# Attention of a two-block model on one core: values stationary, turned weights as the moving operand, one of three head groups in the other row half

## The reference, cut to what matters

```python
# first block, per layer: 3 groups of 8 heads of 64, group g dilated by 1, 4, 16
logits = einsum(q, k) * 64 ** -0.5 + bias; masked outside the window and off the stride
m = max(logits); p = exp(logits - m); s = sum(p); o = (p @ v) / s; lse = m + log(s)
alpha = softmax over the 3 groups of lse;  o = sum_g alpha_g * o_g     # 8 heads x 64
# second block: 16 query heads of 64 on 4 key/value heads, a window of 3 chunks of 64,
sc = q @ k.T * 64 ** -0.5 + bias;  p = softmax([sc, sink])[..., :-1];  o = p @ v
```

## Time and profile before

| | |
|---|---|
| median of 3 runs | 2090.59 us (2090.15 to 2091.51) |
| profiled execution, span | 2088.1 us (no other time is given of it) |
| TensorE busy | 99% |
| VectorE / ScalarE busy | 69% / 49% |
| block 1's attention | about 342 to 461 us and 1059 to 1173 us |
| block 2's attention | about 1682 to 1792 us |

### The profile page before, as it was taken

One profiled execution on the slowest core, in us unless ns is written; L12 is line 12 of the kernel. 1 busy time (PEld: TensorE's weight loads), 2 busy tenths in 40 slices (PEclk: granted clock), 3 DMA queues, 4 the chain that ended last, 5 costly groups with the idle time before them and its releaser, 6 DMA issues.

```text
span 2088.1 us, 28981 instructions
## 1 busy us (share of the span) xinstructions
PE 2057.4 (99%) x11649; PEld 1788.4 (86%) x11649; DVE 1432.8 (69%) x1822; ACT 1028.6 (49%) x1279; POOL 36.5 (2%) x78
## 2 busy tenths in 40 slices
PE   7999999999999999999999999999999999999998
PEld 7788888999888888888899998888788799998887
DVE  5887787668777677767866786455654568756454
ACT  4443544444544363445444445444644668646443
POOL 0000000000000000000000000000000010000000
PEclk9999999999999999999999999999999999999999
DMA  9887688447688758868865485654755454456652
GB/s 320 269 286 249 194 287 249 128 145 252 222 263 264 247 164 280 263 202 260 288 185 144 144 300 194 199 188 144 228 195 182 137 161 137 162 184 210 195 188 81
DMA packets 355929, 438.04 MB, mean 210 GB/s; under 512 B 9571, under 2 KB 323371, under 8 KB 355796
## 3 DMA queue, kind: packets, MB, share of 16 engines
q1 hardware_dynamic: 350592, 420.51, 61.8%
q0 software_dynamic: 4160, 14.23, 3.1%
q10 hardware_dynamic: 1044, 1.46, 0.2%
HBM read 435.05 MB, written 1.11 MB: 209 GB/s over the span
## 4 chain that ended last, share of the span: by engine, by line
PE 86%; DVE 6%; ACT 4%; DMA 2%; issue 1%; DVEq 1%; SPq 0%; ACTq 0%
PE PC L1808 7%; PE PC L1810 7%; PE PC L1809 6%; PE PA L1808 6%; PE PA L1810 6%; PE PA L1809 6%; PE PB L1808 6%; PE PB L1810 6%; PE PB L1809 6%; PE PA L1801 4%; PE PA L1802 4%; PE PA L1803 4%; PE PC L1839 3%; DVE lo L1172 2%; PE PC L1801 2%; PE PC L1976 2%
## 5 line engine op out<-in xcount | busy, mean ns | idle before, releaser
L1172 DVE TENSOR_TENSOR lo<-raw,hi 128x2048 fp32r<-128x2048 f32 x274 | 626.7, 2289 | 209.3 <-ACT hi L696 208.4
L696 ACT ACTIVATE hi<-raw 128x2048 fp32r<-128x2048 f32 x277 | 529.2, 1911 | 260.5 <-PE PC L1810 115.2
L1198 DVE SCALAR_TENSOR_TENSOR acc<-raw,cs,acc 128x256 f32<-128x256 f32 x448 | 217.1, 485 | 34.4 <-issue 0.9
L1808 PE MATMUL PA<-hi,nn 128*128 128x512 f32 (+1 forms) x528 | 210.0, 398 | 6.7 <-DVE nn L1274 5.6
L1801 PE MATMUL PA<-nn,hi 128*128 128x256 f32 x720 | 209.0, 290 | 0.4 <-ACT f L1089 0.4
L1810 PE MATMUL PA<-hi,nn 128*128 128x512 f32 (+1 forms) x528 | 205.6, 389 | 0.0
L1809 PE MATMUL PA<-lo,nn 128*128 128x512 f32 (+1 forms) x528 | 205.1, 388 | 0.0
L1802 PE MATMUL PA<-nn,lo 128*128 128x256 f32 x720 | 203.6, 283 | 0.0
L1803 PE MATMUL PA<-nn,hi 128*128 128x256 f32 x720 | 203.5, 283 | 0.0
L1808 PE MATMUL PB<-hi,nn 128*128 128x512 f32 x400 | 157.5, 394 | 0.6 <-DVE nn L1274 0.6
L1810 PE MATMUL PB<-hi,nn 128*128 128x512 f32 x400 | 156.0, 390 | 0.0
(11 more groups left out here) (317 smaller groups left out, 4086.8 us busy)
## 6 DMA issues: line engine op xcount, KB each, us to landing
raw<-in_w_in SPq DMA_DIRECT2D x90, 1024.0 KB, 5.3
raw<-in_ada_w SPq DMA_DIRECT2D x66, 1024.0 KB, 7.2
raw<-in_ffn_w_gate SPq DMA_DIRECT2D x88, 512.0 KB, 4.1
raw<-in_ffn_w_up SPq DMA_DIRECT2D x88, 512.0 KB, 5.2
raw<-in_ffn_w_down SPq DMA_DIRECT2D x44, 1024.0 KB, 5.3
raw<-in_ffn_w SPq DMA_DIRECT2D x88, 512.0 KB, 4.8
raw<-in_ffn_w SPq DMA_DIRECT2D x22, 1024.0 KB, 4.9
raw<-in_w_o SPq DMA_DIRECT2D x12, 1024.0 KB, 6.4
```

Source lines behind the costliest of these rows:

```text
L696: A(parts_of(n)[0], raw[:, n % 3, :], ACT.Copy).then_inc(hi_done, 1)
L1172: V.tensor_tensor(l, raw[:, n % 3, :], h.bitcast(F32), ALU.subtract).then_inc(lo_done, 1)
L1198: i = V.scalar_tensor_tensor(o, w[:, k, :], cs[:, k:k + 1], o, ALU.mult, ALU.add)
L1808: MM(o, xl, wh[:, c0:c0 + w], start=first, stop=False, skip_group_check=True)
```

## The change

The logits of group 1 (the middle one) are computed in the other row half of the array: the 256-column units of w_in that make its q and k have each pair of 64-column blocks exchanged when they are split (`raw_of`, `paired`), and its logits go to the other PSUM bank. A step is now a tile and a head in another order: chunk j has the first tile of heads 2j and 2j+1, then their second tile. DVE divides the exponentials by their sum before they are turned (`normalise`). The turned weights of two steps lie in two buffers (the second reaches into the memory of the last chunk of `oL1`), and the product has the values stationary (128 rows, 64 columns) and the turned weights moving (128 columns), the two heads side by side in two column halves, so that the output comes out turned: `otok`, its transposes and their PSUM tile are gone. The orders of all engines follow.

```diff
+SLOTS = (0, 2, 1)
+SWAPPED = [BASE[s] + 6 + n for s in (1, 4) for n in range(4, 8)]
+def tile_at(block, s):
+    return s // 2 % 2 if block == 1 else s % 2
+def width(block, s):
+    return (1 + tile_at(block, s)) * P
+def head1(s):
+    return 2 * (s // 4) + s % 2
...
+        with ExitStack() as r:
+            oL1 = sb("oL1", [P, 4, T], F32R, r)
+        pT_more = sb("pT_more", [P, 4 * T])
...
+            pT = sb("pT", [P, 768 + 512], F32, r)
...
-            otok = sb("otok", [P, 2, 2, P], F32, r)
...
+        def weights_t(s, b0, b1):
+            if s % 2 and b0 >= 4:
+                return pT_more[:, 768 + (b0 - 4) * P:768 + (b1 - 4) * P]
+            return pT[:, s % 2 * 768 + b0 * P:s % 2 * 768 + b1 * P]
...
+        def raw_of(n):
+            w = raw[:, n % 3, :]
+            if n in SWAPPED:
+                return w.rearrange("p (m e f) -> p m e f", e=2, f=HD)[:, :, ::-1, :]
+            return w
...
-                A(parts_of(n)[0], raw[:, n % 3, :], ACT.Copy).then_inc(hi_done, 1)
+                A(paired(n, parts_of(n)[0]), raw_of(n), ACT.Copy).then_inc(hi_done, 1)
...
@@ ACT @@
+            def weights_out(blk, st0, s):
+                nb = len(parts(blk, s)) * width(blk, s) // P
+                act.wait_ge(t_done, st0 + s + 1)
+                if s >= 2:
+                    act.wait_ge(av_done, st0 // 2 + s // 2 if blk == 1 else 16 + s - 1)
+                if nb == 6 and s % 2:
+                    A(weights_t(s, 4, 6), PT[:, 4 * P:6 * P], ACT.Copy)
+                    nb = 4
+                A(weights_t(s, 0, nb), PT[:, 0:nb * P], ACT.Copy).then_inc(pt_done, 1)
...
@@ ACT, chunk j @@
+                    if j:
+                        weights_out(1, st0, 4 * j - 1)
+                    exps(1, st0, 4 * j)
+                    if j:
+                        chunk_high(l * 4 + j - 1, j - 1, oH1)
+                    exps(1, st0, 4 * j + 1)
+                    weights_out(1, st0, 4 * j)
                     if j:
                         conv_high(j - 1)
                     after(c)
                     A(f1[:, :], prod[0], ACT.Copy).then_inc(cv_act, 1)
                     split(c + 3)
...
@@ DVE @@
+            def normalise(blk, st0, s):
+                dve.wait_ge(ex_done, st0 + s + 1)
+                if blk == 1:
+                    V.reciprocal(rinv[:, 0:1], ssum[:, s % 4, 0:1])
+                    dve.drain()
+                    L = S[:, s % 2, 0:3 * w]
+                    V.tensor_scalar(L, L, rinv[:, 0:1], None, ALU.mult).then_inc(nm_done, 1)
...
@@ TensorE @@
+            def attend(t, groups, last):
+                o = OB[:, t * P:(t + 1) * P]
+                for n, blocks in enumerate(zip(*groups)):
+                    for e, (v, p) in enumerate(blocks):
+                        i = MM(o[e * HD:(e + 1) * HD, :], v, p, start=n == 0, stop=n == last, skip_group_check=True)
+                i.then_inc(av_done, 1)
+            def attend1(st0, l, pair):
+                pe.wait_ge(pt_done, st0 + 2 * pair + 2)
+                if pair % 2 == 0 and pair:
+                    pe.wait_ge(ol_done, l * 4 + pair // 2)
...
@@ TensorE, chunk j @@
                     for u in range(3):
                         arrive(c + u)
                         half(c + u, prod[u], 0, nh, nl)
...
+                        if u == 0:
+                            if j:
+                                turn_weights(1, st0, 4 * j - 1)
+                            logits(1, st0, 4 * j)
+                        elif u == 1:
+                            turn_weights(1, st0, 4 * j)
+                            logits(1, st0, 4 * j + 2)
+                        else:
+                            attend1(st0, l, 2 * j)
+                            turn_weights(1, st0, 4 * j + 2)
                         half(c + u, prod[u], 1, nh, nl).then_inc(unit_done, 1)
+                        if u == 0:
+                            if j:
+                                attend1(st0, l, 2 * j - 1)
+                            logits(1, st0, 4 * j + 1)
+                        elif u == 1:
+                            turn_weights(1, st0, 4 * j + 1)
+                            logits(1, st0, 4 * j + 3)
...
@@ TensorE, block 2 @@
+                p, r = divmod(hu, 3)
+                if r == 0 and 1 <= p <= 8:
+                    turn_weights(2, 32, 2 * p - 1)
+                    attend2(2 * p - 2)
+                if r == 1 and 1 <= p <= 8:
+                    attend2(2 * p - 1)
+                if r < 2 and p < 8:
...
+                    logits(2, 32, 2 * p + r)
+                if r == 2 and p < 8:
+                    turn_weights(2, 32, 2 * p)
```

More of the change, by code:

```diff
@@ L368, in build @@
         OB = PC[:, 1024:1280]
-        OT = PC[:, 1280:1536]
         RA = PB[:, 512:1024]
@@ L473, in parts @@
             if block == 1:
-                h = s // 2
-                return [(q1, g * 4 + h // 2, (h % 2) * HD, k1, g * 4 + h // 2, g * 512 + h * HD)
-                        for g in range(3)]
+                h = head1(s)
+                return [(q1, g * 4 + h // 2, ((h + (g == 1)) % 2) * HD, k1, g * 4 + h // 2, g * 512 + h * HD)
+                        for g in SLOTS]
             hp = s // 2
@@ L885, in ffn @@
                 hidden_tile(NG - 1, 1)
[L887 to L907, removed]
@@ new lines, in exps @@
+            def exps(blk, st0, s):
+                act.wait_ge(lg_done, st0 + s + 1)
+                if blk == 1:
+                    L = S[:, s % 2, 0:3 * width(1, s)]
+                    A(L, L, ACT.Exp, bias=negm[:, s % 4, 0:1], accum_out=ssum[:, s % 4, 0:1]).then_inc(ex_done, 1)
+                else:
+                    for e in range(2):
+                        i = A(logits2(s)[:, e, :], logits2(s)[:, e, :], ACT.Exp,
+                              bias=negm[:, s % 4, e:e + 1], accum_out=ssum[:, s % 4, e:e + 1])
+                    i.then_inc(ex_done, 1)
@@ new lines, in turn_weights @@
+            def turn_weights(blk, st0, s):
+                pe.wait_ge(nm_done, st0 + s + 1)
+                if s >= 1:
+                    pe.wait_ge(pt_done, st0 + s)
+                w = width(blk, s)
+                nb = w // P
+                for b in range(len(parts(blk, s)) * nb):
+                    c0 = b * P if blk == 1 else b // nb * (w + 1) + b % nb * P
+                    i = nc.tensor.transpose(PT[:, b * P:(b + 1) * P], S[:, s % 2, c0:c0 + P], ident[:, :])
+                i.then_inc(t_done, 1)
@@ new lines, in attend @@
+            def attend(t, groups, last):
[8 more added lines that the diff above has]
+                    pe.wait_ge(ol_done, l * 4 + pair // 2)
+                nb = 1 + pair % 2
+                groups = [[(v1[:, kb, part[5]:part[5] + HD], weights_block(e, g * nb + kb))
+                           for g, part in enumerate(parts(1, 2 * pair + e)) for kb in range(nb)] for e in range(2)]
+                attend(pair % 2, groups, 3 * nb - 1)
@@ L2017, in tail, with attend2 @@
+            def attend2(s):
+                pe.wait_ge(pt_done, 32 + s + 1)
+                if s % 2 == 0 and s:
+                    pe.wait_ge(ol_done, 8 + s // 2)
+                nb = 1 + s % 2
+                groups = [[(v2[:, kb, part[5]:part[5] + HD], weights_block(s, e * nb + kb))
+                           for kb in range(nb)] for e, part in enumerate(parts(2, s))]
+                attend(s % 2, groups, nb - 1)
             def tail(s, at, units, banks, oH, oL, wide_, first_unit, nka, taken, first_yc=None):
```

256 lines of the change are left out of this document (104 added, 152 removed).

## The result

The changed kernel takes **2068.51 us** (median of 4 runs, 2067.64 to 2068.91) where the kernel before takes 2090.77 (4 runs, 2090.15 to 2091.51): a ratio of 0.9892, 95% interval 0.9880 to 0.9904, or 22.3 us less. Forecast were 2066, range 2060 to 2088. The profiled execution is the one of 2067.64, with a span of 2065.8 us against 2088.1.

A forecast was written before the change was run, and what follows sets the result against it. TensorE, busy 99%, was taken to bound block 1, with three engines level in block 2. Terms -23.2 - 1.2 + 0.1 = -24.3 us took the span from 2088.1 to 2063.8; plus 2.5 gave 2066 us, range 2060 to 2088.

The forecast's parts named there:

- Middle group: Block 1's logits: the other row half leaves four records in sequence instead of six, -10.4 us; exchanged blocks add nothing.
- Values stationary: Block 1's output products: two heads in different column halves overlap as row halves do, 29.6 to 18.7 us, -10.9 us.
- rival B: Output products: column halves take turns instead of overlapping, +20.6 us, 2087 us; chance 0.14.
- The model's fixed part: Logits and products on TensorE: each group costs a fixed 0.21 us for first weight load and emptying, plus its streams.
- Rival A: Output products: weight loads are not taken ahead and wait for the stream, +16 us, 2082 us; chance 0.12.
- Rival C: Output products: each matmul of the other half empties the array first, +50 us, 2116 us; chance 0.08.
- The chunk: One chunk of block 1's attention, four steps, falls from 28.78 us by 2.90 us, -23.2 us for eight.
- the ends of the chunk loops: Behind each block 1 loop, a turn and wide pair fill some 0.6 us of TensorE's wait per layer, -1.2 us.
- Division: DVE ahead of the turn in block 1: passes of about 427 and 598 ns, +0.9 us a chunk, hidden by DVE's idle third.
- Block 2: Block 2's attention: work -1.9 us, stalls of 0 to 5 us before the narrow product taken as 2, together +0.1 us.
- Rival D: Block 2 stalls at every step, 16 at 0.6 us instead of 2 us in all, +8 us, 2074 us; chance 0.06.
- Outside: Stages before, between and behind the attention stages: no change forecast, 0 us.

The follow-up runs named there:

- One column half: Changed kernel with both heads' products written to the same 64 partitions, so the second head's output is misplaced; 2084.80 us.
- the seven reorderings: Changed kernel with ACT's or DVE's lists in block 2 reordered (low part, bank copies, split, high part, recurrence, loop end), alone or together; 2065.89 to 2084.04 us.
- the best order found: Changed kernel with low part early, high part ahead of bank copies, and ACT's old order in block 2's last four half units; 2066.43 us, block 2 at 206.10.

## Why the prediction was right, and where it was off

**Middle group, -10.4.** Right in mechanism and size: 0.64 and 1.05 from start to start, and 10.1 us when undone. That nothing is added for the exchanged blocks was right too: 2279 to 2293 ns for a split on DVE, and 952 ns for the wide addition of logits (959 in the earlier trace rows).

**Values stationary, -10.9.** Right, and this was the term that no row could decide. With 0.80 and 1.46 the pairs cost 18.1 us in block 1 against the 18.7 worked out and the 34.2 of rival B. The model's fixed part is smaller here, 0.16 to 0.18 for 0.21: the second load of a product starts 0.05 us after its first (371.93, 371.98), that of block 2's logits 0.10 after the earlier trace rows. One column half gives back 15.1 us of it, as B has it. Rival A (loads wait for the stream) would have spaced two records by 0.21; they are spaced by 0.11. Here the rule of the Trainium skill (TensorE: Matmul & The Clock Gate, The mechanism), that a load overlaps matmuls in flight only where the row group differs, disagrees with the measurement: both heads' tiles lie in the same rows and their loads are hidden. The same section also lets a load go ahead when it targets the background weight buffer; that would fit, but no run here shows which buffer a load takes. The other rule (TensorEngine Tiling (Array Packing), Key Properties), that different tiles load and multiply in parallel, agrees for column halves, as 1.46 against 2.77 us shows. What the prediction didn't have is the condition: side by side in the queue. Without the alternation of heads 0.92 of the 1.31 us that the halves save in a wide pair are gone. Rival C (an emptied array for each matmul) needed 0.27 us a matmul of two records; it is 0.12 (1.46 / 12).

**The chunk, 28.78 to 25.88.** Measured 25.78: eight chunks -24.0 for -23.2. Both layers together gave 24.8 for 24.4, so the ends of the chunk loops gave 0.8 where I had 1.2. TensorE's waits behind layer 1's loop (0.4 and 0.2 us in the kernel before) are gone altogether, so what is missing lies in the work at the ends of the loops; where, was not traced.

**Division, hidden in block 1.** Right: leaving it out changes neither layer by more than 0.03 us. Its passes were put at 427 and 598 ns and take 420 and 621:

```profile
L1521 DVE TENSOR_SCALAR S<-S,rinv 128x768 f32<-128x768 f32 x16 | 9.9, 621 | 1.2
L1521 DVE TENSOR_SCALAR S<-S,rinv 128x384 f32<-128x384 f32 x16 | 6.7, 420 | 1.6 <-issue 0.4
```

**Block 2, +0.1.** Measured +0.96, and that it is so near is luck: two terms were both too small and nearly cancel. The work: a chunk without stalls is 0.51 us shorter, so -4.1 for eight, where the step said -1.9; I had counted the change between product and logits twice, once in the product's fixed part and once as 0.09 of its own, and had 0.42 and 0.64 for products that take 0.37 and 0.59. The stalls: I took 2 us and at most 5, at one place, the narrow product behind the low part. There they are 4.5 us in seven waits, near the upper end. But with gates and queries the waits are 7.1 in all against 2.7 before, +4.4; read from start to start they grew by 6.0. With the -4.1 of the work that makes +0.3 to +1.9, and the measured +0.96 lies between. The step that failed is the one on what stands behind the moved work in ACT's and DVE's queues: it followed the product and its low part, and left out that exponentials waiting for a later logit also hold up the bank copies behind them. Rival D (0.6 us at every one of 16 steps, 9.6 in all) didn't come either: at its places there are seven waits of at most 0.9 us.

**The cause of the stalls** is only partly shown. Shown is that the low part's place in the lists sets the 4.5 us (moved, they are gone), that the bank copies' place sets the others, and that the division counts (without it -4.5), by its time in DVE's list or on the path. Shown as well is that freeing one moves most of the wait elsewhere: six of the seven reorderings gained 1.2 us or less in this block, or lost. What the best order would give is open; the best here is 206.1 us. The new order of steps, the two weight buffers and the missing turn of the output were not undone one by one; for them the chunk's timeline stands alone.

**Outside, 0.** Measured +1.2 ahead of block 2. The unchanged stage above differs by 2.4 us between two profiles of the same code, so nothing of the change is needed for it. Together: the forecast span of 2063.8, - 0.4 (block 1), + 0.9 (block 2), + 1.2 (outside) and + 0.3 behind the last turn of the residual make the 2065.8 of the profile. The time lies 1.8 above its span there, where I allowed 2.5, and the median another 0.9 above that execution: 2068.5.

## What to carry to other kernels

Two products that fill half of the columns each can run as one when they lie in different column halves and are issued in turns; issued head after head, most of it is lost, though nothing else differs. A stage in which TensorE is full pays out what its own work loses, here to 0.4 us in 24; a stage in which three engines run level paid out nothing here before its lists were reordered, and 1.9 us of 208 with the best order found, and each reordering has to be traced to what then stands last in each in-order list, the table loads included. Price such a stage by its whole lists, not by the one hand-over that the change touches, and read its gain and its new waits separately: here -4 and +4 to +6 looked like a quiet +1.

## What the runs showed of the hardware

- Overlap of two column halves reaches over four records at a seam: 0.39 us saved with the heads issued one after the other, at both lengths (2.77 to 2.38, 1.46 to 1.07).
- A change of mode costs about 0.09 us once, whichever way: 0.21 from a plain record to the product where 0.12 is usual, 0.20 from the product's last record to the logits (64 rows) where its rounds are 0.11 apart, in block 1 (373.19 to 373.39) and in block 2 alike, and 0.20 from the product to the turns. Between two groups of different halves it is paid once, not for leaving and for entering.
- A table load stands in ACT's timeline with 1.28 us, 1.30 from its start to the next activation's; the copy of the high part at 1775.02 needs none. The Trainium skill (ScalarE activation tables: per-element evaluation and per-set limits, What a function is on this engine) has 1283 ns for it, between two functions of different sets, and the 1.28 agrees.
- The same code in a stage that nothing touched (the one of 185.55 us above) took 184.4 to 188.2 us in the profiles of these runs. The three longest, 187.9 to 188.2, all have a stretch of 30 us at a mean granted clock of 0.94; the others reach 186.0 at 1.00. Either is as much as the effects of 1 us that were looked for in block 2; those could be told only stage by stage.
